# A two-layer backbone on one core: two ring parts loaded through other modulation slots, a reciprocal applied at the copy, norms by token part

## What is computed

```python
def diff_attn_block(q, k, v, lam):                    # layer 0, four heads
    s = einsum("mbhqd,mbhkd->mbhqk", q, k) * 64 ** -0.5
    p = softmax(s, axis=-1)
    w = p[0] - lam * p[1]
    return einsum("bhqk,bhkd->bhqd", w, v)            # then rmsnorm over 128

for i in range(2):
    mod_l = split(silu(c) @ ada_w[i] + ada_b[i], 6)    # shift, scale, gate, shift, scale, gate
    h_l = rmsnorm(x_l, norm_mix_g[i]) * (1 + mod_l[1]) + mod_l[0]
    o_l = even_mixer(h_c, h_l) if i == 0 else fourier_mix(h_l, w_fnet)
    x_l = x_l + mod_l[2] * o_l
    f_l = rmsnorm(x_l, norm_ffn_g[i]) * (1 + mod_l[4]) + mod_l[3]
    x_l = x_l + mod_l[5] * grouped_moe(f_l)           # router, 2 of 16 experts per token
return rmsnorm(x_l, final_g)
```

## Time and profile before

| | us |
|---|---|
| three runs | 993.85, 996.31, 996.83 |
| median | 996.31 |
| the profiled execution | 998.04 |
| its span | 996.2 |
| mean granted TensorE clock, share of full | 0.896 |

### The profile page before, as it was taken

How to read it: one execution, slowest core, us unless ns; L and a number is a source line. 1 busy time by engine, 2 the same in 40 slices (tenths; PEclk the granted TensorE clock), 3 DMA queues, 4 the chain that set the end, 5 groups by cost and what they waited for, 6 DMA issues and landing times.

```text
span 996.2 us, 18127 instructions
## 1 busy us (share of the span) xinstructions
PE 824.4 (83%) x6940; PEld 441.4 (44%) x6941; DVE 390.6 (39%) x882; ACT 179.4 (18%) x385; POOL 37.9 (4%) x63
## 2 busy tenths in 40 slices
PE   8899899988989968986659976899869879697590
PEld 3544646444554434543325532374435445254240
DVE  3267879858978742111102210423611111121113
ACT  3221010316430201111101110421111111111101
POOL 0000000120001010000000000100010000000001
PEclk9699989998979988998779987899979989798795
DMA  9899877999307888689999899892779999999943
GB/s 339 289 351 352 321 255 275 358 358 310 130 1 257 343 350 331 248 317 414 418 415 417 324 415 351 297 379 90 293 296 411 371 414 416 415 417 413 417 167 134
DMA packets 102841, 320.54 MB, mean 322 GB/s; under 512 B 12944, under 2 KB 28176, under 8 KB 86288
## 3 DMA queue, kind: packets, MB, share of 16 engines
q1 hardware_dynamic: 78432, 282.84, 72.5%
q0 software_dynamic: 4592, 21.41, 5.8%
q10 hardware_dynamic: 19776, 15.75, 4.9%
HBM read 303.58 MB, written 24.64 MB: 329 GB/s over the span
## 4 chain that ended last, share of the span: by engine, by line
PE 33%; issue 28%; DMA 13%; SPq 11%; DVE 9%; ACT 2%; ACTq 1%; POOL 1%; DVEq 0%; POOLq 0%
PE bank L1472 7%; SPq L475 6%; DMA raw<-in_w_up 5%; DMA arena<-unit_rows 4%; PE bank L1408 4%; PE bank L1694 4%; PE bank L1614 3%; PE bank L1803 3%; SPq L444 3%; DMA ring<-in_w_in 2%; PE bank L1476 2%; PE bank L1707 2%; PE bank L1481 1%; SPq L460 1%; DVE arena L879 1%
## 5 line engine op out<-in xcount | busy, mean ns | idle before, releaser
L1694 PE MATMUL bank<-raw,arena 128*32 128x256 f32 x3392 | 250.3, 437 | 73.0 <-DMA raw<-in_w_up 44.3
L1694 PEld LDWEIGHTS bank<-raw,arena 128*32 128x32 f32 x3392 | 119.7, 122 | 183.3 <-DMA raw<-in_w_up 61.1
L1290 DVE TENSOR_TENSOR arena<-arena,bank 64x256 f32<-64x256 f32 x53 | 22.5, 424 | 358.9 <-ACT arena L788 358.9
L1707 PE MATMUL bank<-raw,arena 128*32 128x256 f32 x1696 | 110.5, 387 | 0.8 <-DVE arena L1278 0.8
L1707 PEld LDWEIGHTS bank<-raw,arena 128*32 128x32 f32 x1696 | 59.4, 113 | 40.0 <-issue 3.8
L1472 PE MATMUL bank<-ring,arena 128*128 128x512 f32 x160 | 70.0, 594 | 0.3 <-DMA ring<-in_w_in 0.3
L879 DVE SCALAR_TENSOR_TENSOR bias<-ring,small,bias 128x512 f32<-128x512 f32 x84 | 63.2, 752 | 3.0
L1681 PE MATMUL bank<-consts_sb,arena 64*128 64x64 f32 x212 | 36.0, 292 | 33.9 <-DVE arena L1290 29.9
L788 ACT ACTIVATE arena<-bank 64x256 f32<-64x256 f32 x53 | 19.9, 376 | 238.1 <-PE bank L1694 208.6
L1408 PE MATMUL bank<-consts_sb 128*128 128x512 f32 x132 | 61.9, 616 | 0.0
L1681 PEld LDWEIGHTS bank<-consts_sb,arena 64*128 64x128 f32 x212 | 28.5, 193 | 43.9 <-DVE arena L1290 33.7
(11 more groups left out here) (238 smaller groups left out, 815.5 us busy)
## 6 DMA issues: line engine op xcount, KB each, us to landing
raw<-in_w_gate SPq DMA_DIRECT2D x64, 1024.0 KB, 19.2
raw<-in_w_up SPq DMA_DIRECT2D x64, 1024.0 KB, 21.0
raw<-in_w_down SPq DMA_DIRECT2D x64, 1024.0 KB, 22.2
ring<-in_ada_w SPq DMA_DIRECT2D x24, 2048.0 KB, 13.1
ring<-in_w_in SPq DMA_DIRECT2D x7, 2048.0 KB, 14.3
unit_results<-arena ACTq DMA_DIRECT2D x244, 32.0 KB, 7.2
arena<-unit_rows ACTq DMA_DIRECT2D x55, 128.0 KB, 6.9
ring<-in_w_out SPq DMA_DIRECT2D x2, 2048.0 KB, 41.5
```

The costliest lines, as they stand in the source:

```text
L1694: ins = mm(ps[4][o:o + S, 0:FW], xT[:, i, j * S:(j + 1) * S], w[:, k % 4, h * FW:(h + 1) * FW], start=(k == 0), stop=(k == KD - 1))
L1707: ins = mm(ps[5][j * S:(j + 1) * S, 0:XW], hT_e[:, k % QN, k // QN * S:(k // QN + 1) * S], w[:, k % 2, j * XW:(j + 1) * XW], start=(k == 0 ...
```

## The change

1. `AT1` and `ORDER`: layer 1's modulations lie at other places of `mods`, so that slots 16 and 17 are free after layer 1's first norm; these two slots are loaded ahead of the last eight parts instead of behind them.
2. Attention: the first reciprocal is kept in `inv` and goes into ScalarE's two instructions on the output as their scale. The second weight is the first sum times the second reciprocal times lambda's factor. The scaling pass is left to the mLSTM steps alone.
3. Norms: square, mean, root and reciprocal of each token part by itself. Ahead of the experts, the gate copies and the scaled gain stand before the residual (`mix_in`), token part 0 is normed before part 1's last residual half, the scaling pass writes without a stride into `squares`, and only the shift pass writes with one. The large memset comes last.
4. `keep_busy(14, 7)` goes, and `keep_busy(2, 7)` is `keep_busy(5, 7)`.
5. The output is stored token part by token part.
6. TensorE's loop over the experts is placed so that its head is at slot 0 of a block of the program.

```diff
--- before.py
+++ after.py
@@ -220,7 +220,7 @@
 
         MODS = 11776
         mods = arena[:, MODS:MODS + 7 * D].rearrange("p (a n) -> p a n", a=7)
-        AT1 = [2, 3, 0, 1, 5, 6]
+        AT1 = [4, 5, 0, 1, 2, 3]
         mod1, mod0 = [mods[:, a, :] for a in AT1], mods[:, 3:7, :]
         SC = [5, 6, 3, 4]
 
...
@@ -398,7 +399,7 @@
         fill_of = {c: n // RING + 1 for n, c in enumerate(STREAM)}
         MAIN = 2 * RING
         ORDER = [list(range(RAWS)),
-                 [10, 11, 0, 1, 2, 3, 4, 5, 6, 7, 8, 9] + list(range(MAIN, RAWS))]
+                 [10, 11, 0, 1, 2, 3, 4, 5, MAIN + 4, MAIN + 5, 6, 7, 8, 9] + list(range(MAIN, MAIN + 4))]
...
@@ -518,14 +519,18 @@
                 sp.dma_start(slot(FNET_AT + hf), fnet_v[:, :, hf * W:(hf + 1) * W]).then_inc(fnet_in[hf], 16)
 
             def fnet_used(s):
-                norm_used(1, s)
+                if s == MAIN + 4:
+                    sp.wait_ge(h_ready, 8)
+                elif s < MAIN + 4:
+                    norm_used(1, s)
                 if s == 2 * FNET_AT:
                     sp.wait_ge(mix_ps, 8)
 
             load_experts(1, fnet_used)
-            sp.wait_ge(h_ready, H_FIN)
-            sp.dma_start(out.rearrange("(t p) d -> p t d", p=P), f_).then_inc(stored, 16)
-            sp.wait_ge(stored, 16)
+            for t in range(TT):
+                sp.wait_ge(h_ready, H_FIN - TT + t + 1)
+                sp.dma_start(out[t * P:(t + 1) * P, :], f_[:, t, :]).then_inc(stored, 16)
+            sp.wait_ge(stored, 16 * TT)
...
@@ -707,8 +712,9 @@
                 if it < 8:
                     act.wait_ge(o_ps, it + 1)
                     h, t = it // 2, it % 2
-                    nc.scalar.copy(mg[:, t, h * HD:(h + 1) * HD], ps[7][:, 0:HD])
-                    nc.scalar.activation(mx["xcst"][:, 224:352], ps[7][:, 0:HD], ACT.Square,
+                    first = inv[:, 2 * it:2 * it + 1]
+                    nc.scalar.activation(mg[:, t, h * HD:(h + 1) * HD], ps[7][:, 0:HD], ACT.Identity, scale=first)
+                    nc.scalar.activation(mx["xcst"][:, 224:352], ps[7][:, 0:HD], ACT.Square, scale=first,
                                          accum_out=oss[:, it:it + 1]).then_inc(o_used, 1)
...
@@ -741,10 +747,10 @@
                     root_table(k)
                 for t in range(TT):
                     x_wait(t)
-                    nc.scalar.activation(arena[:, JUNK + t * D:JUNK + (t + 1) * D], xl[:, t, :], ACT.Square,
+                    nc.scalar.activation(squares[:, t, :], xl[:, t, :], ACT.Square,
                                          accum_out=ssq[:, t:t + 1]).then_inc(sq_ready, 1)
-                act.wait_ge(ms_ready, k + 2)
-                nc.scalar.activation(rstd[:, 0:TT], rstd[:, 2:2 + TT], ACT.Sqrt).then_inc(root_ready, 1)
+                    act.wait_ge(ms_ready, 3 + 2 * (k - 2) + t + 1)
+                    nc.scalar.activation(rstd[:, t:t + 1], rstd[:, 2 + t:3 + t], ACT.Sqrt).then_inc(root_ready, 1)

...
@@ -1082,8 +1079,9 @@
                 o = 2 * (it % 2)
                 dve.wait_ge(prob, 2 * it + 2)
                 if it < 8:
-                    link(nc.vector.reciprocal(att[:, 4 + o:6 + o], att[:, 4 + o:6 + o]))
-                    link(nc.vector.tensor_tensor(att[:, 5 + o:6 + o], att[:, 5 + o:6 + o], lam_s[:, 5:6], ALU.mult))
+                    link(nc.vector.reciprocal(inv[:, 2 * it:2 * it + 2], att[:, 4 + o:6 + o]))
+                    link(nc.vector.tensor_scalar(att[:, 5 + o:6 + o], att[:, 4 + o:5 + o],
+                                                 inv[:, 2 * it + 1:2 * it + 2], lam_s[:, 5:6], ALU.mult, ALU.mult))
                 else:
                     dve.wait_ge(s_free, it - 8 + 1)
                     dve.wait_ge(expm, it - 8 + 1)
@@ -1092,7 +1090,7 @@
                     link(nc.vector.tensor_tensor(att[:, 4 + o:6 + o], att[:, 4 + o:6 + o],
                                                  att[:, 12 + o:14 + o], ALU.max))
                     link(nc.vector.reciprocal(att[:, 4 + o:6 + o], att[:, 4 + o:6 + o]))
-                link(nc.vector.tensor_scalar(E_[:, o, :], E_[:, o, :], att[:, 4 + o:5 + o], None, ALU.mult))
+                    link(nc.vector.tensor_scalar(E_[:, o, :], E_[:, o, :], att[:, 4 + o:5 + o], None, ALU.mult))
                 nc.vector.scalar_tensor_tensor(E_[:, o, :], E_[:, o + 1, :], att[:, 5 + o:6 + o], E_[:, o, :],
                                                ALU.mult, ALU.add).then_inc(wc_ready, 1)
 
...
+            def scaled_gain(n, scale, wait_gain):
+
+                dve.wait_ge(*wait_gain)
+                nc.vector.scalar_tensor_tensor(scale, scale, 1.0, gain[:], ALU.add, ALU.mult).then_inc(gain_used, 1)
+                dve.wait_ge(gain_used, n)
+
+            def norm(n, t, g, shift, by_k=False):
+
+                at = 2 * (n - 2) + t
+                dve.wait_ge(sq_ready, NT + at + 1)
+                nc.vector.tensor_scalar(rstd[:, 2 + t:3 + t], ssq[:, t:t + 1], 1.0 / D, EPS, ALU.mult, ALU.add
+                                        ).then_inc(ms_ready, 1)
+                dve.wait_ge(root_ready, 3 + at + 1)
+                link(nc.vector.reciprocal(rstd[:, 4 + t:5 + t], rstd[:, t:t + 1]))
+                even = squares[:, t, :] if by_k else f_[:, t, :]
+                ins = nc.vector.scalar_tensor_tensor(even, xl[:, t, :], rstd[:, 4 + t:5 + t], g, ALU.mult, ALU.mult)
+                if shift is not None:
+                    link(ins)
+                    if by_k:
+                        ins = nc.vector.tensor_tensor(f_kd[t], even.rearrange("p (m k) -> p m k", k=KD),
+                                                      shift.rearrange("p (m k) -> p m k", k=KD), ALU.add)
+                    else:
+                        ins = nc.vector.tensor_tensor(even, even, shift, ALU.add)
+                ins.then_inc(h_ready, 1)
+
+            def mix_in(l, gate, scale, shift, out_gate, wait_gain):
+
+                n = 2 + 2 * l
                 nc.vector.memset(runA, 0.0)
                 nc.vector.memset(runB, 0.0)
                 for j in range(JN):
-                    ins = nc.vector.tensor_copy(gate_s[j * S:(j + 1) * S, :], gate[j * S:(j + 1) * S,
-                                                                                   j * XW:(j + 1) * XW])
-                link(ins)
+                    nc.vector.tensor_copy(gate_s[j * S:(j + 1) * S, :], out_gate[j * S:(j + 1) * S,
+                                                                                 j * XW:(j + 1) * XW])
+                scaled_gain(n, scale, wait_gain)
+                for q in range(3):
+                    residual(4 * l, q, gate)
+                dve.wait_ge(mix_used, 4 * l + 3)
+                norm(n, 0, scale, shift, True)
+                residual(4 * l, 3, gate)
+                dve.wait_ge(mix_used, 4 * l + 4)
+                norm(n, 1, scale, shift, True)
+                nc.vector.memset(ys, 0.0).then_inc(L[l]["y_ready"], 1)
 
             def route(l):
 
@@ -1349,14 +1350,15 @@
                             link(ins)
                     ins.then_inc(added, 1)
 
-            residual(0, [0, 1, 2, 3], mod0[:, 0, :])
             dve.wait_ge(mod_ready, 8)
-            prepare(0, mod0[:, 3, :])
-            norm_mod(2, 4, mod0[:, 2, :], mod0[:, 1, :], (gain_in, 32), by_k=True)
+            mix_in(0, mod0[:, 0, :], mod0[:, 2, :], mod0[:, 1, :], mod0[:, 3, :], (gain_in, 32))
             route(0)
             experts(0)
             combine_results(0)
-            norm_mod(3, 5, mod1[1], mod1[0], (gain_late, 16), 8 + 2)
+            dve.wait_ge(mod_ready, 8 + 4)
+            scaled_gain(3, mod1[1], (gain_late, 16))
+            for t in range(TT):
+                norm(3, t, mod1[1], mod1[0])
...
             dve.wait_ge(mod_ready, 8 + N_ADA)
-            residual(4, [0, 1, 2, 3], mod1[2])
-            prepare(1, mod1[5])
-            norm_mod(4, 6, mod1[4], mod1[3], (gain_late, 32), by_k=True)
+            mix_in(1, mod1[2], mod1[4], mod1[3], mod1[5], (gain_late, 32))
             route(1)
             experts(1)
             combine_results(1)
-            norm_mod(5, 7, None, None, (gain_late, 48))
+            dve.wait_ge(gain_late, 48)
+            for t in range(TT):
+                norm(5, t, gain[:], None)
...
-                keep_busy(14, 7)
                 for t in range(TT):
                     if t:
-                        keep_busy(2, 7)
+                        keep_busy(5, 7)
                     pe.wait_ge(h_ready, 2 * (2 + 2 * l) + t + 1)
                     for b in range(2):
                         for k in range(4):
...
-                with pe.Fori(0, ROUNDS) as r:
+                with nc.Fori(0, ROUNDS, engines=bass.OrderedEngineSet([pe.engine]), head_slot={pe.engine: 0}) as r:
                     for a in range(1, HELD + 1):
                         prev, own = held(a - 1, r), held(a % HELD, r + a // HELD)
                         n_tok = pe.value_load(cnt_i[0:1, bass.ds(r * HELD + a, 1)], min_val=0, max_val=SEQ)
```

55 lines of the change are left out of this document (10 added, 45 removed).

## The result

The changed kernel takes 983.40 us in the median (six runs, 980.77 to 993.18), the kernel before 996.26 (six runs, 991.92 to 996.83). The ratio is 0.9878 with a 95% interval of 0.985 to 0.9906, so the change saves 9 to 15 us. Forecast were 985.2 us, in a range from 979.5 to 991.5. The profiled execution took 985.22, with a span of 983.4 us; the one before had 996.2.

A forecast was written before the change was run, and what follows sets the result against it. Layer 1's expert weight stream, full at 410 GB/s, was taken as the bound, so an earlier start counts fully. Seven terms sum to -11.15 us: 998.04 to 986.9 profiled, median 1.73 lower, 985.2; range 979.5 to 991.5.

The forecast's parts named there:

- e: Layer 1's norm ahead of the experts: earlier norm and removed fillers let part 1's transposes start sooner, -7.8 us.
- f: Layer 1's scatter: slots 16 and 17 loaded sooner leave four weight parts, not six, ahead of it, -3.0 us.
- Rival 1: Layer 1's scatter is slow by itself, so f gives 0 and the time is 988.2 us; chance 0.13.
- h: Last norm and store: output normed and stored token part by part, -1.6 us, ends -0.4 and -2.2.
- b: Layer 0's norm: TensorE idles without fillers, then runs at slow clock; part 1 transposed at 344.3, not 343.76, +0.5 us.
- Rival 2: Layer 0 gives more back: slow clock until the router, +3.4 us more, 988.6 us; chance 0.10.
- a: Attention: VectorE drops a pass over the weights eight times, of which not all comes back, -1.9 us.
- d: Layer 1's first norm: ScalarE is free later, so TensorE's third sum and the Fourier part start later, +1.05 us.
- g: Instruction fetches: the placed loop head brings a TensorE stall in layer 1's expert 2, layer 0 unchanged, +1.6 us.
- Rival 4: Expert loop's code is fetched again at each return, slower; 1008 us with four uncovered returns; chance 0.02.

The follow-up runs named there:

- e5: Changed kernel with the 14 fillers put back ahead of token part 0's transposes in both layers, five between the parts staying: 996.18 us, 0.9994 of the kernel before.
- e6: Kernel before with only its fillers as in the changed one (none ahead of part 0, five between the parts): 1003.55 us, ratio 1.0069.
- e1: Changed kernel with layer 1's loads as before (AT1 and ORDER put back, slots 16 and 17 late again): 988.11 us, 0.9902 of the kernel before.
- e2: Kernel before with only layer 1's loads as in the changed one (slots 16 and 17 loaded sooner): 992.88 us, ratio 0.9947.
- e7_strided: Changed kernel with the scaling pass of the norms ahead of the experts writing with its stride again: 987.41 us, 0.9901 of the kernel before.
- e10: Kernel before run once more, unchanged, for a second trace of it: 997.96 us in one run.
- e9: Changed kernel with the attention as before (reciprocal applied by VectorE's pass over the weights): 985.98 us, 0.9905 of the kernel before.
- e11: Changed kernel with three fillers ahead of step 14's transposes in the attention's tail: 984.86 us, 0.9901 of the kernel before.
- e12: Changed kernel with three attention-tail fillers, nine in layer 0, and layer 1's first-norm scaled gain made earlier: 983.09 us, 0.9846 of the kernel before.
- e3: Changed kernel without the placing of the loop's head (plain loop of before): 987.23 us, 0.9888 of the kernel before.

## Why the prediction was right, and where it was not

The forecast was a sum of seven terms, -11.15 us; the two traces differ by 12.8 in span, the ratio by 12.2 (9.4 to 14.9). By its own steps:

- **e, layer 1's norm and fillers, -7.8:** right, S3 is 7.8 less. Part 1 was turned at 6.7 us behind the mix, where 6.5 to 8.5 had been named. Its reason holds as well: TensorE's 14 fillers and VectorE's late norm had covered one another, and only both together move the stage (e5, e6).
- **f, the scatter, -3.0:** right, S4 is 3.0 less, and e1 and e2 show that it comes from the bytes ahead of it. Over all traces S4 is 5.3 with the new loads (nine) and 8.7 with the old (five), so 3.4 would have been nearer; to expert 1's begin it is 3.3 (10.9 for 14.2), and 2.4 in the two profiles. Rival 1 is out.
- **h, the last norm and store, -1.6:** mis-sized. S6 is 1.9 less in the two profiles and 2.3 less as a mean of all (17.1 in five traces, 14.8 in nine), nearer to the far end, -2.2. Its own two pieces, 0.45 for the passes and 1.3 for the store, are 1.75, not 1.6. The store came as priced: from the last pass's end to the end of the span it is 4.4 to 4.5 us with one store and 3.0 to 3.1 with two, 1.4 less. The step that failed is the passes: from the last gather to their end it is 12.6 as a mean of the five and 11.8 of the nine (12.5 and 12.0 in the two profiles), 0.9 less for 0.45. Which part of the new order does that, no run takes apart.
- **b, layer 0, +0.5:** right in reason, a little small: S2 is 0.9 longer in the two profiles. The slow clock behind TensorE's idle time (8.25 us) is what the prediction priced, and the transposes (1.97) and five fillers (6.20) took what it had written, 2.1 and 6.1. As it had said, these slow fillers (until 342.0) were last, and not VectorE, which had part 1 ready at 340.4. What was short is the distance between the two transposes, 7.4 us in the prediction (336.9 to 344.3) and 7.8 in the trace (334.02 to 341.82). Rival 2, a slow clock until the router, did not come: the router's first matmuls take 1.07, as before.
- **a, the attention, -1.9:** mostly not there. (Its own terms, 0.5 and five times 0.3, are 2.0.) S1 is 2.4 less in the two profiles, which looks like a hit, and the second trace of before takes it away. The step that failed is how much comes back of what VectorE drops, which had been priced as all but TensorE's limit of 0.3 a step: 0.5 us come back from the first to the eighth step, and 0.6 to 0.9 to the end of the sums at the same clock. And the tail behind it lasts 1.0 to 2.2 us longer where the clock falls, which the prediction had not in it at all.
- **d, layer 1's first norm, +1.05:** wrong, 0. From the last gather of layer 0 to the last mix matmul of layer 1 it is 60.3 to 61.0 us in five traces with the old norm and 60.2 to 61.1 in nine with the new one. The failed step is ScalarE: it had its second root at 638.84 and then waited 0.77 us for TensorE's sums, which stand behind TensorE's own fillers. I had priced a late ScalarE without asking when its work would come.
- **g, the fetches, +1.6:** right in place and length (1.53 for 1.70), wrong in price. No cost is seen: S5 is as long without it. I had noted that the stream still waits for experts there, and read it as a reason for a cost; the wait for weights behind it, as far as the traces tell, takes it back.

So the terms that were real and in the two profiles are e, f, h and b: -7.8 -3.0 -1.9 +0.9 = -11.8, within the 9.4 to 14.9 that were measured. Of the three others (-1.9, +1.05, +1.6) the first was a third to a half of its size and two were nothing, and it is luck that they sum to +0.75. What else the two profiles differ in has no edit behind it that a run shows: S1 -2.4, most of it of the profile before alone; S5 +2.5 (240.9 before; beside it only e7_strided is low, with 241.8); layer 0 from part 1's transposes to the last gather, 286.2 before and 284.0 after, in which the stream of weights runs from 248.5 to 254.5 us in the fourteen traces; and +0.8 in the first norm and the Fourier part, +0.7 from the rows' load to expert 1's begin, -0.5 ahead of the attention. With these the 12.8 us of the two spans are complete. The spread of the weight stream is larger than most terms here.

Rival 4, the loop fetched again at each return, did not occur: there are 26 instruction packets for 25, and at the returns after the first no stall on "issue" above 0.6 us in either layer. The Trainium skill, "Runtime: NRT & Kernel Launch", section "Instruction fetch mechanics", says that a taken branch to code outside a window of two pages forces a fetch. By it each of the returns would have stalled. The fourteen traces do not agree: each has 25 to 27 instruction packets, and a stall at a return only at the first one of layer 0, 3.8 to 5.7 us in twelve of them.

## What to carry to other kernels

A filler, and the work that it covers, must be judged as a pair: taking the fillers away alone cost 7 us of the whole time here, the early norm with the fillers left in place gave nothing (in part by estimate), and both together gave 7.8 us in layer 1's norm. A transfer that someone waits for should not stand behind transfers nobody waits for yet; count the bytes ahead of it at the moment of its issue and move those that have an idle stretch elsewhere. And before terms of 1 to 3 us are read from the difference of two traces, take a second trace of the unchanged kernel: here two of its stretches moved by 2.6 and 2.7 us, in opposite directions, with no edit at all. A stretch that spreads can still be read in pieces, if traces with the same granted clock are put side by side.

## What the runs showed of the hardware

- One gap of 3.03 us of TensorE in the attention's tail, in the same code of the old attention, went with a granted clock of 1.00 over the 6 us around it in two executions (e2, e6) and of 0.81 and 0.72 in two others (e10, e9); with the gap filled to 0.41 us it was 1.00 (e11, e12). In layer 0 the transposes behind gaps of 8.25 and 8.02 us took 1.97 us both times, the five fillers behind them 6.20 and 5.25.
- Four indirect scatters, issued within 4 us, took 4.6 to 5.8 us from their last issue to the next load when four weight parts stood ahead of them (nine traces), and 8.4 to 9.3 when six did (five).
- A VectorE pass over 128x1024 float32 that scales, by two factors, took 1.96 to 2.02 us where it wrote neighbours 128 elements apart, and 1.28 to 1.29 where it wrote without a stride; the plain addition of the shift took 1.89 to 1.97 with the strided write and 1.22 to 1.23 without.
- Stalls of TensorE on nothing but "issue" moved with the loop's place: 1.2 to 2.1 us in the middle of layer 1's expert 2 in all eight traces with the head placed, none there in four of the six without, and 3.1 and 3.2 ahead of expert 2 in the two others (e6, e3). S5 was 243.5 in e3 and 245.3 in e6, and in the mean no longer with the head placed (243.5) than without (243.4).
